# A gated hybrid decoder layer on one core: a weight sum moved forward, merges that add from the banks, and GpSimd's late low parts in operations of 256 columns

## What is computed

```
proj   = x @ w_in + b_in                  # 13 parts: qa fa ia za | qb kb vb zb | qi ki wi | ga gb
ua     = (rmsnorm(hgrn2(qa, fa, ia)) * norm_a_g * silu(za)) @ w_up_a
ub     = (topk_attention(qb, kb, vb, qi, ki, wi) * silu(zb)) @ w_up_b
merged = sigmoid(ga) * ua + sigmoid(gb) * ub
y      = merged @ w_out
out    = layer_norm(ALPHA * x + y, ln_g, ln_b)
```

## Time and profile before

| | us |
|---|---|
| median of 3 runs | 463.41 |
| the profiled execution | 463.86 |
| its span (first to last instruction) | 461.9 |
| TensorE busy | 448.9 (97%) |
| DVE busy | 319.4 (69%) |
| ACT busy | 236.7 (51%) |
| GpSimd busy | 185.3 (40%) |

### The profile page before, as it was taken

The page is one execution under the profiler, slowest core; times in us unless marked ns, Lnnn a source line. Parts: engine busy times, 40 slices in busy tenths (PEclk is TensorE's granted clock), DMA queues, the critical chain, the costliest instruction groups (busy, mean ns, idle before and its releaser), DMA issues.

```text
span 461.9 us, 7700 instructions
## 1 busy us (share of the span) xinstructions
PE 448.9 (97%) x2946; PEld 365.5 (79%) x2946; DVE 319.4 (69%) x585; ACT 236.7 (51%) x398; POOL 185.3 (40%) x173
## 2 busy tenths in 40 slices
PE   9999999999999999999999999999999999979993
PEld 7778888888888888888888887887888888757782
DVE  4446589999999843447989975960720079789977
ACT  5735454263346655376697485725873523534421
POOL 0444442582259724571013000000074486535972
PEclk9999999999999999999999999999999999988998
DMA  8808222266024620214020312050136352240013
GB/s 265 285 17 291 74 76 92 91 159 206 0 92 106 172 88 1 92 27 157 1 92 3 122 67 89 3 184 0 58 125 258 107 182 93 91 180 3 0 45 136
DMA packets 16724, 47.73 MB, mean 103 GB/s; under 512 B 2441, under 2 KB 4273, under 8 KB 16177
## 3 DMA queue, kind: packets, MB, share of 16 engines
q1 hardware_dynamic: 16448, 47.05, 30.6%
q10 hardware_dynamic: 240, 0.20, 0.2%
HBM read 43.04 MB, written 2.11 MB: 98 GB/s over the span
## 4 chain that ended last, share of the span: by engine, by line
PE 84%; DVE 9%; POOL 2%; issue 2%; ACT 2%; DVEq 0%; POOLq 0%
PE bank L627 21%; PE bank L628 21%; PE bank L629 20%; PE bank L788 2%; PE bank L773 2%; POOL w_lo L2058 2%; PE bank L871 2%; PE bank L824 2%; DVE s_lo L1749 1%; DVE z_a L1770 1%; DVE mix L1723 1%; PE bank L764 1%; PE bank L763 1%; PE bank L954 1%; PE bank L957 1%
## 5 line engine op out<-in xcount | busy, mean ns | idle before, releaser
L1984 POOL TENSOR_TENSOR w_lo<-w_raw,w_hi 128x512 fp32r<-128x512 f32 x84 | 113.1, 1373 | 160.0 <-ACT w_hi L965 160.0
L627 PE MATMUL bank<-x_hi,w_hi 128*128 128x512 f32 x336 | 133.0, 396 | 0.0
L628 PE MATMUL bank<-x_lo,w_hi 128*128 128x512 f32 x336 | 131.2, 390 | 0.0
L629 PE MATMUL bank<-x_hi,w_lo 128*128 128x512 f32 x336 | 130.9, 390 | 0.0
L627 PEld LDWEIGHTS bank<-x_hi,w_hi 128*128 128x128 f32 x336 | 63.1, 188 | 13.9 <-issue 0.8
L629 PEld LDWEIGHTS bank<-x_hi,w_lo 128*128 128x128 f32 x336 | 63.1, 188 | 13.6
L628 PEld LDWEIGHTS bank<-x_lo,w_hi 128*128 128x128 f32 x336 | 63.1, 188 | 12.1
L965 ACT ACTIVATE w_hi<-w_raw 128x1024 fp32r<-128x1024 f32 (+2 forms) x63 | 62.4, 1011 | 7.2 <-PE bank L629 4.1
L1052 ACT ACTIVATE prob<-prob,nmax 128x128 f32<-128x128 f32 (+3 forms) x32 | 17.7, 555 | 41.5 <-DVE nmax L1505 41.5
L1481 DVE MAX8 best<-score 128x8 f32<-128x256 f32 (+2 forms) x48 | 26.8, 559 | 1.0
L1493 DVE COPY prob_t<-bank 128x128 f32<-128x128 f32 (+3 forms) x32 | 14.2, 486 | 19.0 <-PE bank L773 18.9
(11 more groups left out here) (269 smaller groups left out, 846.6 us busy)
## 6 DMA issues: line engine op xcount, KB each, us to landing
w_raw<-in_w_units SPq DMA_DIRECT2D x58, 512.0 KB, 4.6
w_raw<-in_w_units SPq DMA_DIRECT2D x2, 1024.0 KB, 4.7
y_sb<-in_x_tok SPq DMA_DIRECT2D x4, 512.0 KB, 4.9
out<-y_sb SPq DMA_DIRECT2D x8, 256.0 KB, 2.0
x_raw_hi<-in_x_t SPq DMA_DIRECT2D x4, 256.0 KB, 4.5
x_raw_lo<-in_x_t SPq DMA_DIRECT2D x4, 256.0 KB, 6.4
t_turned<-t_row SPq DMA_DIRECT2D x1, 1024.0 KB, 9.8
q_hi_g<-q_hi_g SPq DMA_DIRECT2D x8, 128.0 KB, 3.7
```

The lines of the kernel that those rows point to most:

```text
L627: nc.tensor.matmul(dst, a_hi, b_hi, start=first, stop=False)
L628: nc.tensor.matmul(dst, a_hi, b_lo, start=False, stop=False)
L629: return nc.tensor.matmul(dst, a_lo, b_hi, start=False, stop=last)
L1984: nc.gpsimd.tensor_tensor(split_target(u, kiwi_lo, x_lo, w_lo)[:, k, :], raw(u)[:, k, :], split_target(u, kiwi_hi, x_hi, w_hi)[:, k, :].bi ...
```

## The change

1. Loads: b11 and b12 are loaded ahead of up0's weights. b12 is loaded a second time, into z_a, once b11's low part and t1 are made.
2. t1 is made in z_b at q = 106, ahead of merge 0. t2 then follows in z_b and t3 in z_a.
3. In merge the product of gate a stays in the bank, and the add reads it there. The fills with even numbers now wait for the add (mix_done) in place of the product.
4. GpSimd's low parts of up1, up2, up3 and of the output weights are made in operations of 256 columns, two where there was one.
5. DVE makes only the first half of t1's low part; GpSimd makes the other half, behind b21's.
6. ACT rounds b21 behind the sum of merge 4, and runs keep_first(1) ahead of the last round_sums.

```
-OUT_HI_AT = {109: ((0, 0),), 110: ((0, 1),), 117: ((1, 0),), 118: ((1, 1),), 120: ((2, 0), (2, 1))}
-OUT_LO_AT = {110: 0, 119: 1}
-T1_AT, T1_LO_AT = 115, 121
+OUT_HI_AT = {109: ((0, 0),), 110: ((0, 1),), 120: ((2, 0), (2, 1))}
+OUT_HI_THEN = {118: ((1, 0), (1, 1))}
+OUT_LO_AT = {110: ((0, 0), (0, 1), (0, 2), (0, 3)), 119: ((1, 0), (1, 1), (1, 2), (1, 3)), 121: ((2, 2), (2, 3))}
+T1_AT, T1_LO_AT = 106, 121
...
             for u in range(2, NMAIN):
+                if UNITS[u] == "up0":
+                    sp.wait_ge(o_lo_done, 4)
+                    load_out("b11", z_a[:])
+                    load_out("b12", z_b[:])
...
-                if UNITS[u] == "up1":
-                    sp.wait_ge(o_lo_done, 4)
-                    load_out("b11")
-                    load_out("b12")
...
+            wait_out_lo(sp, 0, 4)
+            sp.wait_ge(out_sum, 1)
+            load_out("b12", z_a[:])
...
-                else:
-                    pe.wait_ge(up_out[fill % 4], fill // 4)
+                elif fill % 2:
+                    pe.wait_ge(up_out[fill % 4], fill // 4)
+                else:
+                    pe.wait_ge(mix_done, fill // 2 - 1)
...
+                for n, half in OUT_HI_THEN.get(q, ()):
+                    split_out_hi(n, half)
             split_out_hi(4, 0)
             split_out_hi(4, 1)
             round_merged(KT - 1)
             keep_first(0)
+            keep_first(1)
             round_sums(PAIRS - 1)
-            keep_first(1)
...
-                nc.vector.tensor_tensor(mx, up_bank[fa][:], gate_tiles(m, 1)[:, 0, :], ALU.mult).then_inc(up_out[fa], 1)
+                a_gated = up_bank[fa][:]
+                nc.vector.tensor_tensor(a_gated, a_gated, gate_tiles(m, 1)[:, 0, :], ALU.mult).then_inc(a_done, 1)
                 nc.vector.tensor_tensor(gb, up_bank[fb][:], gb, ALU.mult).then_inc(up_out[fb], 1)
...
-                nc.vector.tensor_tensor(mx, mx, gb, ALU.add).then_inc(mix_done, 1)
+                nc.vector.tensor_tensor(mx, a_gated, gb, ALU.add).then_inc(mix_done, 1)
...
             def first_sum_lo():
-                hi, lo = out_weights(2)
-                nc.vector.tensor_tensor(lo, out_raw("t1"), hi.bitcast(F32), ALU.subtract).then_inc(out_lo_dve, 1)
+                hi, lo = (w[:, 0:2, :] for w in out_weights(2))
+                nc.vector.tensor_tensor(lo, out_raw("t1")[:, 0:2, :], hi.bitcast(F32),
+                                        ALU.subtract).then_inc(out_lo_dve, 1)
...
+                each = 1 if u > UNITS.index("up0") else 2
+                for k in (slice(n, n + each) for n in range(2 * j, 2 * j + 2, each)):
+                    ins = nc.gpsimd.tensor_tensor(split_target(u, kiwi_lo, x_lo, w_lo)[:, k, :], raw(u)[:, k, :],
...
-                hi, lo = (w[:, piece, :] for w in out_weights(n))
-                nc.gpsimd.tensor_tensor(lo, out_raw(name)[:, piece, :], hi.bitcast(F32), ALU.subtract).then_inc(out_lo, 1)
+                for c in (slice(0, HALF), slice(HALF, SEQ)):
+                    hi, lo = (w[:, piece, c] for w in out_weights(n))
+                    ins = nc.gpsimd.tensor_tensor(lo, out_raw(name)[:, piece, c], hi.bitcast(F32), ALU.subtract)
+                ins.then_inc(out_lo, 1)
```

More of the change, by code:

```diff
@@ L298, in hybrid_kernel @@
         out_sum, out_hi, out_lo, out_lo_dve = (sem(n) for n in ("out_sum", "out_hi", "out_lo", "out_lo_dve"))
+        a_done = sem("a_done")
         first_kept, pre_12, pre_21 = sem("first_kept"), sem("pre_12"), sem("pre_21")
@@ L478, in out_raw @@
                 return w_raw[:, ring[name] % 2, :].rearrange("p (j n) -> p j n", j=PAIRS)
-            return z_a[:] if name in ("b11", "t1", "t2") else z_b[:]
+            return z_a[:] if name in ("b11", "t3") else z_b[:]
         def wait_out_raw(eng, name):
@@ L486, in wait_out_raw @@
                 eng.wait_ge(out_sum, ("t1", "t2", "t3", "t4").index(name) + 1)
-        LO_ORDER = (0, 1, 4, 3, 5, 6)
+        LO_ORDER = (0, 1, 2, 4, 3, 5, 6)
         def wait_out_lo(eng, n, pieces):
+            before = 4 * LO_ORDER.index(n) - 2 * (LO_ORDER.index(n) > LO_ORDER.index(2))
             if n == 2:
                 eng.wait_ge(out_lo_dve, 1)
+                if pieces > 2:
+                    eng.wait_ge(out_lo, before + pieces - 2)
             else:
-                eng.wait_ge(out_lo, 4 * LO_ORDER.index(n) + pieces)
+                eng.wait_ge(out_lo, before + pieces)
         HI_ORDER = (0, 1, 2, 4, 3, 5, 6)
@@ L579, in _, with load_out @@
             sp.dma_start(id_sb[:], ident).then_inc(early_in, 16)
-            def load_out(name):
-                sp.dma_start(out_raw(name), w_units[NMAIN - 1 + OUT_BLOCKS.index(name)]
+            def load_out(name, dst):
+                sp.dma_start(dst, w_units[NMAIN - 1 + OUT_BLOCKS.index(name)]
                              .rearrange("p (j n) -> p j n", j=PAIRS)).then_inc(out_in[name], 16)
             for u in range(2, NMAIN):
+                if UNITS[u] == "up0":
+                    sp.wait_ge(o_lo_done, 4)
+                    load_out("b11", z_a[:])
+                    load_out("b12", z_b[:])
                 if u >= 3:
@@ L608, in _ @@
             sp.dma_start(ln_gb[:, 1, :], ln_b.partition_broadcast(P)).then_inc(ln_in, 16)
+            wait_out_lo(sp, 0, 4)
+            sp.wait_ge(out_sum, 1)
+            load_out("b12", z_a[:])
             wait_lo(sp, UNITS.index("up2"), 4)
-            load_out("b21")
+            load_out("b21", out_raw("b21"))
             wait_lo(sp, UNITS.index("up3"), 4)
-            load_out("b22")
+            load_out("b22", out_raw("b22"))
             sp.wait_ge(part_done, parts(UNITS.index("up3"), 1))
@@ L938, in _ @@
                 elif name == "t2":
-                    pe.wait_ge(up_out[i], 2 * KT // 4)
+                    pe.wait_ge(mix_done, KT)
+                    pe.wait_ge(up_out[1], 2 * KT // 4)
                 elif name == "t3":
@@ L1757, in sum_out @@
                     wait_out_raw(dve, "b12")
-                    wait_out_lo(dve, 0, 4)
-                    a, b = out_raw("b12"), out_raw("b11")
+                    a, b = z_b[:], z_a[:]
                 elif name == "t2":
                     wait_out_raw(dve, "b22")
-                    dve.wait_ge(out_lo_dve, 1)
-                    a, b = out_raw("b22"), out_raw("t1")
+                    wait_out_lo(dve, 2, 4)
+                    a, b = out_raw("b22"), z_b[:]
                 elif name == "t3":
-                    a, b = out_raw("b22"), out_raw("b12")
+                    dve.wait_ge(out_in["b12"], 32)
+                    a, b = out_raw("b22"), z_a[:]
                 else:
@@ L1982, in split_lo @@
                 wait_hi(pool, u, j)
-                k = slice(2 * j, 2 * j + 2)
-                nc.gpsimd.tensor_tensor(split_target(u, kiwi_lo, x_lo, w_lo)[:, k, :], raw(u)[:, k, :],
-                                        split_target(u, kiwi_hi, x_hi, w_hi)[:, k, :].bitcast(F32),
-                                        ALU.subtract).then_inc(lo_done, 1)
+                each = 1 if u > UNITS.index("up0") else 2
+                for k in (slice(n, n + each) for n in range(2 * j, 2 * j + 2, each)):
+                    ins = nc.gpsimd.tensor_tensor(split_target(u, kiwi_lo, x_lo, w_lo)[:, k, :], raw(u)[:, k, :],
+                                                  split_target(u, kiwi_hi, x_hi, w_hi)[:, k, :].bitcast(F32),
+                                                  ALU.subtract)
+                ins.then_inc(lo_done, 1)
             def bias_and_penalty(i):
@@ L2069, in _ @@
                 side(q)
-                if q in OUT_LO_AT:
-                    for piece in range(4):
-                        split_out_lo(OUT_LO_AT[q], piece)
-            for n in LO_ORDER[2:]:
+                for n, piece in OUT_LO_AT.get(q, ()):
+                    split_out_lo(n, piece)
+            for n in LO_ORDER[3:]:
                 for piece in range(4):
```

3 lines of the change are left out of this document (1 added, 2 removed).

## The result

The changed kernel takes 459.80 us (median of 4 runs, 459.45 to 460.65) against 463.43 for the kernel before (median of 4 runs beside it): ratio 0.9923, 95% interval 0.9906 to 0.9941. The profiled execution takes 460.08 us, its span is 458.3. The forecast was 461.1 with a range of 456.8 to 463.7.

What follows compares the result with a forecast made beforehand. The end was taken to be set by sum t2's start on DVE, then GpSimd's low parts of t2. The last piece 3.8 us earlier, less 1.5 for the clock, gave 463.41 - 2.3 = 461.1 us, range 456.8 to 463.7.

Steps and rivals of the forecast that it cites:

- S': Start of sum t2 on DVE, counted from the start of merge 0: 52.48 us before, 47.79 in the changed kernel.
- S: Start of sum t2 on DVE behind the last merge, said to set the end: 421.82 before, 417.2 forecast.
- The waits from merge 3 to S: DVE's waits for the ports shared with GpSimd, between merge 3 and sum t2: 7.4 us in all.
- DVE's 20 operations: Those with two SBUF inputs from merge 3 to sum t2, each forecast to wait 0 to 0.55 us for GpSimd.
- The 4.2 up to merge 3: Merge 3 starts 4.2 us earlier: 3.3 from moving t1, 0.9 from halved waits in merges 1 and 2.
- From S to the last piece: From sum t2's start to GpSimd's last low piece of t2: 13.5 us forecast, 12.65 before.
- The clock: TensorE's clock falls at about 427.6 during t2's waits and returns at 433.7, costing 1.5 us.
- 3.8 - 1.5 = 2.3 us: Total gain: t2's last piece 3.8 us earlier, less 1.5 us of slow clock.
- B: Rival: t2's low parts on GpSimd still bound the kernel, but the clock stays up: 459.6 us, chance 0.22.
- C: Rival: DVE meets GpSimd far less, sum t2 starts near 412.5: 454.9 us, 457 half-way; chance 0.18.
- D: Rival: all 20 DVE operations wait in full for the ports, mean wait above 0.5 us: slower, 464.7 us; chance 0.14.
- E: Rival: gain and loss even out, 463.4 us; chance 0.06.

Runs made afterwards that it cites:

- p1: Changed kernel with the add reading two SBUF inputs again and GpSimd's operations back at 512 columns: 463.80 us, ratio 0.9995 to the kernel before.
- u2: Changed kernel with GpSimd's operations back at 512 columns: 460.30 us, ratio 0.9931 to the kernel before.
- u4: Changed kernel with ACT rounding b21 ahead of merge 4's sum again: 461.11 us, ratio 0.9954 to the kernel before.
- o2: Kernel before with only DVE's sums t3 and t4 moved behind the early output rows: 463.16 us, ratio 0.9999.
- x1: Changed kernel with DVE's sums t3 and t4 moved behind the early output rows: 455.73 us, ratio 0.9833 to the kernel before.
- p2: Changed kernel with t1 at its old place and GpSimd's operations back at 512 columns: 462.66 us, ratio 0.9988 to the kernel before.
- o1: Kernel before with GpSimd's late low parts in operations of 256 columns and nothing else: 465.36 us, ratio 1.0045.

## Why the prediction was right

**The bound: right, with less room than it sounds.** Ten kernels keep the time less S' between 410.9 and 412.6, and in the changed kernel TensorE stands for t2's pieces alone. But the prediction counts the gain as the shift of S without saying how near the other path was: in the kernel before, TensorE by its own stands was 0.27 us from setting the end itself, so a change that had moved S alone would have gained an estimated 0.3 us. This one moved merge 6's low part as well, as the prediction laid out. It put the low part 0.9 us ahead of the matmul that asks for it; the trace has 0.2.

**S itself: right, 417.2 predicted, 417.13 found** (416.49 and the 0.64). Merge 3 was put at 386.1 and is at 386.10 on the same clock. The waits from merge 3 to S were laid out as 1.1, 0.8, 2.2, 0.5, 0.7 and 2.2 us, given as 7.4 in all (they add up to 7.5); in the trace they are 1.1, 0.8, 2.6, 0.6, 0.1 and 2.2, 7.3. That the sum is met within 0.1 is partly luck, since merge 5 is 0.4 too low and merge 6 0.6 too high. Had I subtracted the parts of the change from 421.82 (4.2, 1.9, 1.8 and 1.1) and stopped there, S would have come out 4.3 us too early. Counting again who meets whom on the shared ports made the forecast. The count of meetings was too high, though: 14 of DVE's 20 operations wait, not nearly all, and of the 12 row sums 8 take 0.84 to 0.96 us and 4 their bare 0.41 to 0.42, where all were to take 0.9 to 1.0.

**The sizes of the parts: mixed.** Undone one by one, they move S' by 2.19 (t1's place), 2.73 (adds from banks), 1.05 (256 columns), 1.02 (half of t1's low part) and 2.02 (ACT's order); predicted were 4.2 for the first with shorter waits in merges 1 and 2 counted in, 1.9, no own figure, 1.1 and 1.8. The 4.2 up to merge 3 holds (20.93 before, 16.76 now, counted from merge 0), but I gave 0.9 of it to the shorter GpSimd operations. p1 has merge 3 at 17.64 and u2 at 17.03 with 512 columns, so the adds from banks bring 0.6 and the columns 0.3. And the bank form was counted only in merges 5 and 7, from the earlier trace rows; once GpSimd is busy all along, an add from SBUF is held in nearly every merge, which makes it the largest part. The five parts undone one by one add up to 9.0 us of S', where the whole change moves it by 4.69: each is worth more beside the others than alone.

**From S to the last piece: 13.5 predicted, 13.17 found.** The three waits in t2 were given as 2.6, 0.7 and 0.7 us and are 2.30, 0.42 and 0.23; the wait of 0.7 for first_sum is 0.56.

**The clock: right in its cost, partly by luck.** A fall near 427.6, in the middle of the stand, and a return near 433.7 were forecast: 6.1 us low, 3.0 of them behind the last piece, for 1.5 us. It was low from 428.9 to 432.3, 3.4 us. It fell 2.0 us after TensorE had resumed at 426.89, and 2.6 us of it lay behind the last piece, for 1.22 us. The late fall and the short stretch cancel in the part that counts. That it would fall at all was no more than a chance: in u2 and u4 TensorE stood as long and it didn't.

**The sum.** In place of 3.8 - 1.5 = 2.3 us the parts measure 4.17 - 1.22 = 2.95. The other 0.64 of the profiled pair is the opening, which no step of the prediction had.

**The rivals.** B is out by the trace; with the clock up this execution would have been an estimated 1.2 us faster. C fell on its premise: DVE waits for GpSimd at 14 of the 20 operations. D fell on its mean wait, 0.37 us and not 0.55. E would have been 463.4, and the time is 3.6 below it. The Trainium skill ("SBUF — State Buffer", on the two separate sides), cited for D, says that the pair is held for a whole instruction. The rows agree, with one thing more: no row sum waited longer than one operation of GpSimd (0.55 at 256 columns, 1.10 at 512). So in these traces a queue of short operations does not shut DVE out; it comes next each time. The other page named, the Trainium skill's "VectorE: DVE Perf Modes" (on the TRN2 errata), with 62 cycles more for a read of PSUM, isn't borne out by the add: 692 ns with an input in the bank, 692 without when it isn't held. Writing the product to its bank, which no row had shown, takes 0.69 to 0.70, so taking nothing for it was right.

## What to carry to other kernels

When an engine that shares ports becomes free earlier, recount every meeting on the new order rather than adding up the savings of the parts: here three parts together freed DVE for some 6 us by the prediction's sizes (3.3, 1.8 and 1.1) and brought S' 1.3 forward, until the adds were moved to an operand in a bank, where none of the eight was held (0.692 us each). Look for the second path behind the one the chain of waits names, since TensorE's own stands may end within a fraction of a us of it; a remedy for one alone then gives nothing (o2), and the same remedy after the other is shortened gives 4 us (x1). And keep large operations of one engine on the shared ports away from the time in which its neighbour makes the piece that the bound engine is waiting for.

## What was not expected of the hardware

**How regularly an add from two SBUF tiles is held.** I had put the bank form at one or two tenths of a us a merge against GpSimd's short operations. It is the whole held part, 0.53 to 0.55 us, in four of the five merges from merge 3 on, while the add from a bank took 0.692 us in all eight. The wait isn't always saved: in u2 the next operation with two SBUF inputs takes it over in part.

**Equal stands, and the clock falls or doesn't.** In the changed kernel's profiled execution TensorE stood 2.30, 0.42 and 0.23 us in t2, and the clock went to 1.2 GHz. In u4's it stood as long or longer at the same place, and had stood 1.71 us in b11 before, and the clock stayed at 1.00:

```profile
428.74 0.50 PE L965 MATMUL bank<-w_hi,s_hi_hi 128*128 128x512 f32 x1 [2.31 <-POOL w_lo L2075]
430.13 0.50 PE L965 MATMUL bank<-w_hi,s_hi_lo 128*128 128x512 f32 x1 [0.43 <-POOL w_lo L2075]
431.52 0.50 PE L965 MATMUL bank<-w_hi,s_hi_lo 128*128 128x512 f32 x1 [0.42 <-POOL w_lo L2075]
```

```profile
431.00:432.00 1.00, 0.58 (x3) 0.44 (x3) 0.97 (x2) 0.00 (x0) 1.00 (x2) 1.00 0.00 0
```

What the clock did in the other executions is on record only as its mean over the span. It differs within one kernel: the changed kernel's four have 0.996, 0.996, 0.994 and 0.990, at 459.45, 459.53, 460.08 and 460.65 us. So the clock costs more in some executions than in others, and here the order of the times follows it. It isn't what scatters the times everywhere. p1 ran from 461.80 to 464.45 (12 runs), and 11 of the 12 have 0.987 or 0.988; p2's two fastest, 461.49 and 461.70, have 0.988, and the four around 462.5 have 0.993 or 0.994. Nor do stands alone go with scatter: p1, p2 and u2 (459.38 to 461.52, 6 runs) stand and scatter by 2.1 to 2.7 us, while o1, which stands longest (3.7 us), lies within 0.5 (5 runs) and the kernel before (2.8 us) within 1.0 on one chip (23 runs). What scatters p1, p2 and u2 stays open.
